# Scan of layer 0: one wide matmul for four rows of decays, denominators kept in PSUM, means on ScalarE and GpSimd, transposes of the unit matrix in waits

## The chip, the cores and the metric

The kernel runs on one core of a Trainium2 chip. The metric is the device time of one execution, in microseconds (us), as a median over executions. The engines are named as the profile names them: PE (TensorE matmuls), PEld (its weight loads), DVE (VectorE), ACT (ScalarE), POOL (GpSimd) and SP (SyncE, which issues the DMAs).

## The reference

Two layers over 1024 tokens of width 1024, and a last RMS norm. Layer 0 projects the normed tokens and then runs two scans over chunks, an SSD (16 heads of 64, state 128, two groups) and an mLSTM (4 heads, keys of 128, values of 256); layer 1 is an attention with differences of two softmaxes. What the change touches is the scan of layer 0:

```python
# SSD, per chunk
decay = where(causal, exp(a_cs[l] - a_cs[s]), 0)
y_diag = einsum('bclsg,bclsgr,bcsgrp->bclgrp', cb, decay, xdt)
y = y_diag + y_off + xs * d_skip ; y = y * silu(z)
yg = y * rsqrt(mean(y * y, per group of 512) + EPS)
# mLSTM, per chunk
m_t = maximum(inter_log, max(d_log))
w_intra = exp(d_log - m_t) ; w_inter = exp(inter_log - m_t)
den = sum(s) + w_inter * (q . n_mem)
h = num / maximum(abs(den), exp(-m_t))
h = h * sigmoid(o_raw) ; h = h * rsqrt(mean(h * h, per head of 256) + EPS)
...
```

## The kernel before

The program has three parts, one behind the other on every engine. `projection_ab` (to 554 us) forms the features, the gates and their tables. `scan_chunks` works through 8 tiles of 128 tokens (two chunks of 64 each) and then forms the first products with the output weights, the "mid products" (units of 24 matmuls, L1370 to L1372). `layer2` does the remaining mid products, the second layer's projection, the attention and the output product. fp32 products are formed as two or three products of fp32r parts, a high part and a low part.

Each engine has its own instruction order, written out by hand, and waits on semaphores. `S["d_h"]`, say, is counted up by DVE (d) for each finished h. A steady tile n of the scan goes like this:

- PE: the rows of decays of the next tile, four groups of four heads (`decay_rows`, L1074). For each head one matmul with a column of `head_sel` broadcast, 128x128 (L1078), puts that head's row of summed decays on all partitions; a matmul in bf16 of 128x512 (L1080) adds the causal mask to the four of them. The columns come from `chunk_tables` (L1084), which DVE runs once a tile: L1085 copies the tile's scalars into `k_g`, L1087 and L1089 the selecting columns. In the same way the rows of the mLSTM's four heads are put on all partitions: the inter-chunk weights (L1263) and the negative maxima (L1266, mask L1268). In between stand transposes of the features (L1055, L1062, L1064, L1070) and the products of keys and queries (L1280).
- DVE `weights`: copies x and b (L1570, L1573), the first half of the decay weights times the products (L1578), the scaled queries (L1586), st (L1593, PE's next step L1311 needs it), gk, the mean of the SSD's squares of the tile before (L1694), half of the turned outputs (L1619), the other half of the weights (L1578), kg (L1607).
- PE `outputs`: the mLSTM's numerators with the denominators as a 257th column (L1311, L1313), transposes of the tile before (L1292), the state's part (L1325), the diagonal part (L1333), then the memory's and the state's new products (L1342, L1349).
- DVE `outputs`: the denominators (L1637 copies them out of PSUM, L1639 forms the absolute value, L1642 the maximum with exp(-m), L1644 the reciprocal), h (L1650, four), the SSD's y (L1657, L1664), the mean of the squares of h (L1669, behind ScalarE's squares L1426), the next tile's tables (L1085 to L1089), the new memory (L1676) and state (L1687).
- ACT: the exponentials of decays (L1405) and of the mLSTM's weights (L1415), squares of h (L1426) and y (L1443), and the norms' scaling (L1433, L1449).
- POOL: x times dt (L1507), x times the skip (L1511), x at the chunk's end (L1515), the decay of the state (L1522, L1527), the power -1/2 of the means of h (L1531), y plus skip (L1534), y times gate (L1540), the power of the means of y (L1542).

In the last tile DVE forms in addition the low parts of the first output units (`low_y`, L1623) and POOL low parts of weights (L1500). In the rows `k_` marks tensors kept over the parts, `s_` those of the scan, `a_` those of layer 2, `c_` those of a tile's input, `b_w`, `b_y_T`, `b_yy` and the like are shared buffers, and `b_ps` is PSUM.

In `layer2`, `step` (L2465) runs the projection's products; before group 0 PE waits for the normed tokens (`h_ok`). The attention's loop ends with two calls of `turn` and the products L2497 and L2510.

## Time and profile before

| | |
|---|---|
| median of three runs | 1554.47 us (1551.89 to 1555.26) |
| profiled execution | 1556.27 us, its span 1554.6 us |
| mean granted clock of TensorE | 0.991 |
| PE, share of the span busy | 97% |
| DVE | 56% |
| ACT | 43% |
| POOL | 36% |
| chain that ended last, PE's share | 47% |
| projection / scan with its mid products / layer 2 | to 553.8 / to 743.5 / to 1554 us |

The shares are means over three very different parts, so the scan is read from its own stretch: the table by stretches gives the granted clock (1.00 is full speed, 2.4 GHz; 0.50 is 1.2 GHz), and the timeline gives who waits for whom. A row of the timeline merges like instructions that follow each other; a matmul's own time is longer than the distance at which the next one starts, so matmuls are priced by distances of starts.

### The profile page before, as it was taken

How to read it: one execution, taken by the hardware profiler on the slowest of the kernel's cores; microseconds unless marked ns; L12 is line 12 of the kernel's file. 1: busy time of each engine (PE TensorE's matmuls, PEld its weight loads, DVE VectorE, ACT ScalarE, POOL GpSimd, SP SyncE). 2: the span in 40 equal slices, each digit the busy share in tenths (PEclk: the TensorE clock that was granted, in tenths of full speed). 3: DMA queues.
4: the chain of work that ended last, by engine and by line, in shares of the span. 5: the costliest groups of instructions: out<-in, count | busy, mean ns of one | idle time of the engine just before them, and what ended most of it. 6: DMA issues, size and time to landing. Idle time of an engine off the chain costs nothing.

```text
span 1554.6 us, 22919 instructions
## 1 busy us (share of the span) xinstructions
PE 1513.2 (97%) x8742; PEld 1290.6 (83%) x8742; DVE 874.0 (56%) x1430; ACT 672.4 (43%) x1320; POOL 558.6 (36%) x324
## 2 busy tenths in 40 slices
PE   9999999999999999999999999999999999998797
PEld 8798988888999988887788877888888888886686
DVE  7674979595944458886353262445544335553633
ACT  6542534454532245555335343345455333656321
POOL 3245444545444336765555321132121014121110
PEclk9999999999999999999999999999999999999999
DMA  5142333232334365684766320031111012113612
GB/s 181 41 125 93 123 95 122 96 122 95 123 109 136 100 197 173 212 267 156 260 208 217 96 84 28 14 95 48 55 51 57 9 35 75 55 35 115 258 68 109
DMA packets 157296, 176.39 MB, mean 113 GB/s; under 512 B 9736, under 2 KB 130824, under 8 KB 156296
## 3 DMA queue, kind: packets, MB, share of 16 engines
q1 hardware_dynamic: 157048, 174.91, 34.7%
q8 instruction: 68, 1.11, 0.3%
q14 instruction: 36, 0.29, 0.1%
q10 hardware_dynamic: 144, 0.07, 0.0%
HBM read 122.46 MB, written 52.43 MB: 113 GB/s over the span
## 4 chain that ended last, share of the span: by engine, by line
PE 47%; DVE 2%; DMA 1%; issue 1%; ACT 0%; POOL 0%; SPq 0%; POOLq 0%; DVEq 0%; ACTq 0%
PE b_ps L2465 22%; PE b_ps L2510 4%; PE b_ps L2485 4%; PE b_ps L2415 3%; PE b_ps L2417 3%; PE b_ps L2416 3%; PE b_ps L2497 2%; PE b_ps L2567 2%; PE b_ps L2569 2%; PE b_ps L2568 2%; DMA b_yy<-z 1%; PE b_ps L2518 1%; PE b_ps L2433 0%; DMA z<-b_y_T 0%; DVE b_y_T L2256 0%
## 5 line engine op out<-in xcount | busy, mean ns | idle before, releaser
L1986 POOL TENSOR_TENSOR b_w<-b_w_raw,b_w 128x1024 fp32r<-128x1024 f32 x66 | 158.0, 2395 | 359.1 <-DVE b_w L2245 253.7
L2465 PE MATMUL b_ps<-a_h_hi,b_w 128*128 128x512 f32 x768 | 265.8, 406 | 2.8 <-DVE a_h_lo L2223 2.8
L402 POOL TENSOR_TENSOR b_w<-b_y_T,b_w 128x1024 fp32r<-128x1024 f32 x54 | 141.3, 2619 | 172.6 <-ACT b_w L460 172.5
L2465 PEld LDWEIGHTS b_ps<-a_h_hi,b_w 128*128 128x128 f32 x768 | 145.3, 189 | 37.0 <-issue 3.9
L2465 PE MATMUL b_ps<-a_h_lo,b_w 128*128 128x512 f32 x384 | 150.8, 393 | 0.0
L956 PE MATMUL b_ps<-p_hi,b_w 128*128 128x512 f32 x384 | 124.1, 396 | 1.8 <-DVE p_lo L628 1.8
L726 DVE SCALAR_TENSOR_TENSOR b_w_raw<-p_out_raw,k_cols,b_w_raw 128x1024 f32<-128x1024 f32 x60 | 119.7, 2002 | 7.8 <-ACT b_w_raw L492 6.4
L2256 DVE CUSTOM_DVE_ANT_0 b_y_T<-b_ps,a_neg_dist 128x128 f32<-128x128 f32 (+5 forms) x96 | 72.2, 777 | 62.8 <-PE b_ps L2485 52.3
L460 ACT CAST b_w<-b_y_T 128x1024 fp32r<-128x1024 f32 x60 | 62.6, 1044 | 90.6 <-PE b_ps L956 51.2
L963 PE MATMUL b_ps<-b_w,p_hi 128*128 128x256 f32 x576 | 101.8, 281 | 0.0
L2107 ACT ACTIVATE b_y_T<-b_y_T,a_nm 128x128 f32<-128x128 f32 (+5 forms) x96 | 75.3, 785 | 52.9 <-DVE a_nm L2256 52.9
L963 PEld LDWEIGHTS b_ps<-b_w,p_hi 128*128 128x128 f32 x576 | 88.4, 190 | 0.4
L402 POOL TENSOR_TENSOR b_w<-b_y_raw,b_w 128x1024 fp32r<-128x1024 f32 x24 | 61.3, 2554 | 76.2 <-ACT b_w L460 76.2
L956 PEld LDWEIGHTS b_ps<-p_hi,b_w 128*128 128x128 f32 x384 | 72.3, 188 | 17.5 <-issue 1.9
L2510 PEld LDWEIGHTS b_ps<-a_v,a_aT 128*128 128x128 f32 x576 | 75.1, 195 | 11.6 <-ACT a_aT L2117 7.0
L2465 PEld LDWEIGHTS b_ps<-a_h_lo,b_w 128*128 128x128 f32 x384 | 73.0, 190 | 11.8
L2465 PE MATMUL b_ps<-b_w,a_h_hi 128*128 128x512 f32 x256 | 80.9, 397 | 1.2 <-ACT a_v L2095 1.2
L2510 PE MATMUL b_ps<-a_v,a_aT 128*128 128x128 f32 x576 | 76.4, 279 | 5.5 <-ACT a_aT L2117 5.5
L2415 PE MATMUL b_ps<-b_w,a_h_hi 128*128 128x512 f32 x208 | 81.4, 391 | 0.0
L2025 POOL TENSOR_TENSOR a_rs<-a_rs,a_half 128x4 f32<-128x4 f32 x16 | 17.3, 1083 | 177.8 <-DVE a_rs L2282 177.8
L2417 PE MATMUL b_ps<-b_w,a_h_lo 128*128 128x512 f32 x208 | 81.1, 390 | 0.0
L2416 PE MATMUL b_ps<-b_w,a_h_hi 128*128 128x512 f32 x208 | 81.0, 389 | 0.0
(410 smaller groups left out, 3611.6 us busy)
## 6 DMA issues: line engine op xcount, KB each, us to landing
b_y_T<-in_ab_w_in SPq DMA_DIRECT2D x33, 512.0 KB, 4.4
b_w_raw<-in_ab_w_out SPq DMA_DIRECT2D x32, 512.0 KB, 4.2
b_w_raw<-in_c_w_in SPq DMA_DIRECT2D x32, 512.0 KB, 4.1
tok<-p_out_raw SPq DMA_DIRECT2D x48, 256.0 KB, 2.3
feat<-b_w_raw SPq DMA_DIRECT2D x20, 512.0 KB, 2.9
c_fe<-feat SPq DMA_DIRECT2D x7, 1280.0 KB, 6.8
yt<-b_y_T SPq DMA_DIRECT2D x8, 1024.0 KB, 9.7
b_y_raw<-yt SPq DMA_DIRECT2D x32, 256.0 KB, 4.2
```

Source lines behind the costliest of these rows:

```text
L402: gp.tensor_tensor(w_lo[s % SLOTS][:, :, :], operand(n, split_of(n, p))[:, :, :], w_hi[s % SLOTS][:, :, :].bitcast(F32), ALU.subtract).the ...
L726: dve.scalar_tensor_tensor(out=acc, in0=raw(j), scalar=cols[:, c:c + 1], in1=acc, op0=ALU.mult, op1=ALU.add).then_inc(S["tapped" if j < CO ...
L956: mm = pe.matmul(out[:, :], x0[:, k, fs], x1[:, k, :], start=opens and k == 0 and i == 0, stop=closes and k == HK - 1 and i == 2)
L963: mm = pe.matmul(out[:, h * HB:(h + 1) * HB], x0[:, k, ts], x1[:, k, :], start=k == 0 and i == 0, stop=k == HK - 1 and i == 2)
L1986: gp.tensor_tensor(w_lo[:, w, :], w_raw[u % W_RAW][:, :], w_hi[:, w, :].bitcast(F32), ALU.subtract).then_inc(S["l_wlo"], 1)
L2107: nc.scalar.activation(s[:, 0:W], s[:, 0:W], ACT.Exp, bias=nm[n % 2][:, j:j + 1], scale=-1.0, accum_out=sm[n % 2][:, j:j + 1]).then_inc(S[ ...
L2256: dve.tensor_tensor_reduce(s[:, 0:W], score[j][:, at:at + W], neg_dist[:, SEQ - W:SEQ], -SLOPES[h], 3e38, ALU.add, ALU.min, nm[n % 2][:, j ...
L2415: pe.matmul(ps[:, bank, :], y_hi(u)[:, ts], w_hi[:, w, c], start=(k == 0), stop=False)
L2416: pe.matmul(ps[:, bank, :], y_hi(u)[:, ts], w_lo[:, w, c], start=False, stop=False)
L2417: mm = pe.matmul(ps[:, bank, :], y_lo(u)[:, ts], w_hi[:, w, c], start=False, stop=(k == AB_OUT_T - 1))
L2465: mm = pe.matmul(o, x, y, start=(k == 0 and q == 0), stop=(k == KT - 1 and q == 2))
L2510: mm = pe.matmul(ps[:, 5, 0:DA_V], aT[:, k, :], v[:, k, (h % 4) * DA_V:(h % 4 + 1) * DA_V], start=(k == 0), stop=(k == t))
```

## The change

1. One matmul of 128x512 takes the place of four of 128x128 wherever rows of four heads are put on all partitions (L1078, L1263, L1266). The right-hand side becomes block-diagonal: four copies of the rows next to each other, of which copy i keeps only the rows of heads 4q + i (`dec_bd`, `ml_bd`; the mask is `of_four`), so that one column that selects a whole group of four heads gives four rows at once. The selecting columns shrink from 16 and 8 to 4 and 2. `dec_bd` is formed by two DVE operations in the projection (one copy before), `ml_bd` by one at the scan's start, for which PE waits then.
2. The denominators are worked out in PSUM: max(-den, exp(-m)), then max with den in place, then the reciprocal from PSUM; three DVE operations for four.
3. DVE's order: the first L1578 goes behind st and gk. In the last tile the low part of unit 1 goes from the weights to behind y.
4. The means: ScalarE scales inside its squares, GpSimd adds EPS before its powers, and DVE's two operations (L1669, L1694) go. Each square of h waits for its own h and no more for all four.
5. PE gets 62 transposes of the unit matrix into a PSUM bank that nobody reads then (`idle_turns`): 14 and 10 in tile 0 of the scan, 14 before layer 2's group 0, and 12 before each of the attention's last two turns.
6. Buffers: the mLSTM's gate cells get their own, and some scratch of the gates moves; these move no instruction.

```diff
+                dve.tensor_reduce(quads, ident[:, :].rearrange("p (a h) -> p a h", h=ML_HEADS), AX.X, ALU.add).then_inc(S["heads_ok"], 1)
+                dve.tensor_reduce(keep["of_four"][:, :], ident[:, :].rearrange("p (a h) -> p h a", h=ML_HEADS), AX.X, ALU.add
+                                  ).then_inc(S["heads_ok"], 1)
+                dve.wait_ge(S["heads_ok"], 1)
+                of_rows = quads.rearrange("p (r s q) -> p s r q", s=2, q=4)
+                dve.tensor_tensor(keep["heads_of"][:, :, :], of_rows[:, 0, :, :], of_rows[:, 1, :, :], ALU.add).then_inc(S["heads_ok"], 1)
+                of_rows = quads.rearrange("p (b s c) -> p s c b", b=2, s=2)
+                dve.tensor_tensor(keep["cells_of"][:, :, :], of_rows[:, 0, :, :], of_rows[:, 1, :, :], ALU.add).then_inc(S["heads_ok"], 1)
...
-                chain(dve.tensor_copy(dec_rows, g_ps["rows"][:, 2 * P:4 * P].rearrange("p (j t) -> p j t", j=2)))
+                dve.wait_ge(S["heads_ok"], 4)
+                for j in (0, 1):
+                    chain(dve.tensor_tensor(dec_bd[:, j, :, :], mid(g_ps["rows"][:, (2 + j) * P:(3 + j) * P], 4),
+                                            last(keep["of_four"][:, :], P), ALU.mult))
...
 def decay_rows(pe, ps, keep, par, q, S):
     bank = 4 + q % 2
-    for k in range(4):
-        h = 4 * q + k
-        pe.matmul(ps[:, bank, k * P:(k + 1) * P], keep["head_sel"][:, h:h + 1].broadcast_to([P, P]),
-                  keep["dec_rows"][:, par * P:(par + 1) * P], start=(k == 0), stop=False, skip_group_check=True)
+    pe.matmul(ps[:, bank, :], keep["head_sel"][:, q:q + 1].broadcast_to([P, P]), keep["dec_bd"][:, par, :],
+              start=True, stop=False, skip_group_check=True)
     pe.matmul(ps[:, bank, :], keep["ident_bf"][:, :], mid(keep["later"][:, :], 4), start=False, stop=True,
               skip_group_check=True).then_inc(S["p_acs"], 1)
...
-        gates = lambda n, par, i: gz[par][:, i, :] if behind_first(n) else chunk["first_gz"][i]
+        gates = lambda n, par, i: (gz[par][:, i, :] if i < 2 else cell_gate[par]) if behind_first(n) else chunk["first_gz"][i]
...
+        ml_bd = ahead["w"][:, 1, 2, 0:BLK]
...
-                    pe.wait_ge(S["ml_rows"], 4 * 16)
+                    pe.wait_ge(S["d_mlbd"], 1)
                 pe.wait_ge(S["cell_ok"], n + 1)
-                row_of = lambda b, h: keep["cell_sel"][:, ML_HEADS * b + h:ML_HEADS * b + h + 1].broadcast_to([P, P])
+                rows_of = lambda b: keep["cell_sel"][:, b:b + 1].broadcast_to([P, P])
                 if behind_first(n):
                     pe.wait_ge(S["d_cmem"], n * 4)
-                    for k in range(4):
-                        mm = pe.matmul(ps[:, 7, k * P:(k + 1) * P], row_of(1, k), keep["ml_rows"][:, :], start=True, stop=True)
-                    mm.then_inc(S["p_wint"], 1)
-                for k in range(4):
-                    pe.matmul(ps[:, 6, k * P:(k + 1) * P], row_of(0, k), keep["ml_rows"][:, :], start=(k == 0), stop=False,
-                              skip_group_check=True)
+                    pe.matmul(ps[:, 7, :], rows_of(1), ml_bd, start=True, stop=True).then_inc(S["p_wint"], 1)
+                pe.matmul(ps[:, 6, :], rows_of(0), ml_bd, start=True, stop=False, skip_group_check=True)
                 pe.matmul(ps[:, 6, :], ident_bf[:, :], mid(later[:, :], 4), start=False, stop=True,
                           skip_group_check=True).then_inc(S["p_negm"], 1)
                 if not behind_first(n):
                     decays(n, par, 2)
+                    pe.wait_ge(S["d_xtok"], 2)
+                    idle_turns(0, 14)
                     decays(n, par, 3)
+                    idle_turns(0, 10)
                     return
...
+            def idle_turns(bank, count):
+                for _ in range(count):
+                    pe.transpose(ps[:, bank, 0:P], ident[:, :], ident[:, :])
...
-                act.wait_ge(S["d_h"], n * 4 + 4)
-                act.wait_ge(S["d_meanm"], n + 0)
+                act.wait_ge(S["l_meanm"], n + 0)
                 act.wait_ge(S["a_sqy"], n * 2)
                 for h in range(ML_HEADS):
+                    act.wait_ge(S["d_h"], n * 4 + (h + 1))
                     act.wait_ge(S["a_sqm"], n * 4 + h)
-                    nc.scalar.activation(x_sq[:, 0:ML_V], y[:, D + h * ML_V:D + (h + 1) * ML_V], ACT.Square,
+                    nc.scalar.activation(x_sq[:, 0:ML_V], y[:, D + h * ML_V:D + (h + 1) * ML_V], ACT.Square, scale=ML_V ** -0.5,
                                          accum_out=ssq[:, 2 + h:3 + h]).then_inc(S["a_sqm"], 1)
...
-                act.wait_ge(S["d_meany"], n + 0)
+                act.wait_ge(S["l_meany"], n + 0)
                 for k in (0, 1):
                     act.wait_ge(S["a_sqy"], n * 2 + k)
-                    nc.scalar.activation(x_sq[:, :], y[:, k * 512:(k + 1) * 512], ACT.Square,
+                    nc.scalar.activation(x_sq[:, :], y[:, k * 512:(k + 1) * 512], ACT.Square, scale=512 ** -0.5,
                                          accum_out=ssq[:, k:k + 1]).then_inc(S["a_sqy"], 1)
...
-                gp.wait_ge(S["d_meanm"], n + 1)
+                gp.wait_ge(S["a_sqm"], n * 4 + 4)
+                gp.tensor_tensor(rms[:, 2:6], ssq[:, 2:6], eps[:, :], ALU.add).then_inc(S["l_meanm"], 1)
+                gp.wait_ge(S["l_meanm"], n + 1)
                 gp.tensor_tensor(rms[:, 2:6], rms[:, 2:6], half[:, 0:4], ALU.pow).then_inc(S["l_rstdm"], 1)
...
-                gp.wait_ge(S["d_meany"], n + 1)
+                gp.wait_ge(S["a_sqy"], n * 2 + 2)
+                gp.tensor_tensor(rms[:, 0:2], ssq[:, 0:2], eps[:, 0:2], ALU.add).then_inc(S["l_meany"], 1)
+                gp.wait_ge(S["l_meany"], n + 1)
                 gp.tensor_tensor(rms[:, 0:2], rms[:, 0:2], half[:, 0:2], ALU.pow).then_inc(S["l_rstdy"], 1)
...
-                ssd_weights(0)
...
-                means()
+                ssd_weights(0)
...
                     low_y(0)
-                    low_y(1)
...
-                dve.tensor_copy(den[:, :], ps[:, 4:8, ML_V:VW].rearrange("p h a -> p (h a)")).then_inc(S["d_den"], 1)
-                dve.wait_ge(S["d_den"], n * 4 + 1)
-                dve.scalar_tensor_tensor(out=den2[:, :], in0=den[:, :], scalar=-1.0, in1=den[:, :],
+                den_ps = ps[:, 4:8, ML_V:VW].rearrange("p h a -> p (h a)")
+                dve.scalar_tensor_tensor(out=den[:, :], in0=den_ps, scalar=-1.0, in1=g[:, T_EMT:T_EMT + ML_HEADS],
                                          op0=ALU.mult, op1=ALU.max).then_inc(S["d_den"], 1)
-                dve.wait_ge(S["d_den"], n * 4 + 2)
-                dve.tensor_tensor(den2[:, :], den2[:, :], g[:, T_EMT:T_EMT + ML_HEADS], ALU.max).then_inc(S["d_den"], 1)
-                dve.wait_ge(S["d_den"], n * 4 + 3)
-                dve.reciprocal(den[:, :], den2[:, :]).then_inc(S["d_den"], 1)
-                dve.wait_ge(S["d_den"], n * 4 + 4)
+                dve.wait_ge(S["d_den"], n * 3 + 1)
+                dve.tensor_tensor(den_ps, den_ps, den[:, :], ALU.max).then_inc(S["d_den"], 1)
+                dve.wait_ge(S["d_den"], n * 3 + 2)
+                dve.reciprocal(den[:, :], den_ps).then_inc(S["d_den"], 1)
+                dve.wait_ge(S["d_den"], n * 3 + 3)
...
-                dve.wait_ge(S["a_sqm"], n * 4 + 4)
-                dve.tensor_scalar(rms[:, 2:6], ssq[:, 2:6], 1.0 / ML_V, EPS, ALU.mult, ALU.add).then_inc(S["d_meanm"], 1)
-                if not is_last(n):
+                if is_last(n):
+                    low_y(1)
+                else:
                     next_tables()
...
-            def ssd_means(n):
-                dve.wait_ge(S["a_sqy"], n * 2 + 2)
-                dve.tensor_scalar(rms[:, 0:2], ssq[:, 0:2], 1.0 / 512, EPS, ALU.mult, ALU.add).then_inc(S["d_meany"], 1)
+            dve.wait_ge(S["ml_rows"], 4 * 16)
+            dve.tensor_tensor(ml_bd.rearrange("p (h t) -> p h t", t=P), mid(keep["ml_rows"][:, :], 4), last(keep["of_four"][:, :], P),
+                              ALU.mult).then_inc(S["d_mlbd"], 1)
             weights(0, 0, 0)
             def body(n, par, prior):
                 outputs(n, par, prior, lambda: tables(n + 1, prior + par))
-                weights(n + 1, 1 - par, prior + par, lambda: ssd_means(n), lambda: turn(n, 0, par, prior))
+                weights(n + 1, 1 - par, prior + par, lambda: turn(n, 0, par, prior))
...
-            ssd_means(TILES - 1)
...
                     if g == 0:
+                        idle_turns(bank, 14)
                         pe.wait_ge(S["h_ok"], TILES)
...
             for n in range(-1, N + 1):
+                if n >= N - 1:
+                    pe.wait_ge(S["a_fe"], G)
+                    idle_turns(7, 12)
...
-            keep |= dict(heads_of=sel[:, 0:64].rearrange("p (r h) -> p r h", h=SSD_HEADS),
-                         cells_of=sel[:, 64:128].rearrange("p (c h) -> p c h", c=TILES), head_sel=sel[:, 128:128 + SSD_HEADS],
-                         cell_sel=sel[:, 144:144 + 2 * ML_HEADS], ml_rows=sel[:, 152:152 + P])
+            keep |= dict(heads_of=sel[:, 0:16].rearrange("p (r q) -> p r q", q=4),
+                         cells_of=sel[:, 16:32].rearrange("p (c b) -> p c b", c=TILES), head_sel=sel[:, 32:36],
+                         cell_sel=sel[:, 36:38], ml_rows=sel[:, 40:40 + P])
```

PE, tile 0 of the scan, from its first products of keys and queries (L1254) to the diagonal products; `k_sel` are the selecting columns, before:

```order
L1254 MATMUL b_ps<-b_w_raw,b_y_raw 128x128 x4
L1266 MATMUL b_ps<-k_sel 128x128 x4
L1268 MATMUL b_ps<-k_later,k_ident_bf 128x512
L1078 MATMUL b_ps<-k_dec_rows,k_sel 128x128 x4
L1080 MATMUL b_ps<-k_later,k_ident_bf 128x512
L1078 MATMUL b_ps<-k_dec_rows,k_sel 128x128 x4
L1080 MATMUL b_ps<-k_later,k_ident_bf 128x512
L1311 MATMUL b_ps<-c_va,s_st 128x257 x4
```

and now:

```order
L1262 MATMUL b_ps<-b_w_raw,b_y_raw 128x128 x4
L1271 MATMUL b_ps<-b_w,k_sel 128x512
L1272 MATMUL b_ps<-k_later,k_ident_bf 128x512
L1084 MATMUL b_ps<-k_dec_bd,k_sel 128x512
L1086 MATMUL b_ps<-k_later,k_ident_bf 128x512
L1293 MATMUL b_ps<-k_ident 128x128 x14
L1084 MATMUL b_ps<-k_dec_bd,k_sel 128x512
L1086 MATMUL b_ps<-k_later,k_ident_bf 128x512
L1293 MATMUL b_ps<-k_ident 128x128 x10
L1323 MATMUL b_ps<-c_va,s_st 128x257 x4
```

Each four became one of four times the width, and two runs of turns (L1293) stand before and behind the last group. In the later tiles the groups change in the same way and no turns come in.

DVE, a steady tile, from the copies of x to kg, before:

```order
L1570 COPY s_x_tok<-b_ps 128x512 x2
L1573 COPY s_b_tok<-b_ps 128x256
L1578 TENSOR_TENSOR s_wt<-s_dec,b_ps 128x1024
L1586 TENSOR_TENSOR s_qs<-c_fe,b_ps 128x512
L1589 COPY s_c_dec<-b_ps 128x4
L1593 SCALAR_TENSOR_TENSOR s_st<-b_ps,s_wm 128x512
L1596 TENSOR_SCALAR s_gk<-s_wm 128x4
L1694 TENSOR_SCALAR s_rms<-s_ssq 128x2
L1619 TENSOR_TENSOR b_y_T<-b_ps,b_y_T 128x512 x2
L1578 TENSOR_TENSOR s_wt<-s_dec,b_ps 128x1024
L1607 TENSOR_TENSOR s_kg<-b_ps,s_gk 128x512
```

and now:

```order
L1588 COPY s_x_tok<-b_ps 128x512 x2
L1591 COPY s_b_tok<-b_ps 128x256
L1602 TENSOR_TENSOR s_qs<-c_fe,b_ps 128x512
L1605 COPY s_c_dec<-b_ps 128x4
L1609 SCALAR_TENSOR_TENSOR s_st<-b_ps,s_wm 128x512
L1612 TENSOR_SCALAR s_gk<-s_wm 128x4
L1596 TENSOR_TENSOR s_wt<-s_dec,b_ps 128x1024
L1634 TENSOR_TENSOR b_y_T<-b_ps,b_y_T 128x512 x2
L1596 TENSOR_TENSOR s_wt<-s_dec,b_ps 128x1024
L1622 TENSOR_TENSOR s_kg<-b_ps,s_gk 128x512
```

The first half of the weights moved from before the queries to behind gk, and the mean is gone. DVE, the same tile, from the denominators to the memory, before:

```order
L1637 COPY s_den<-b_ps 128x4
L1639 SCALAR_TENSOR_TENSOR s_den<-s_den 128x4
L1642 TENSOR_TENSOR s_den<-s_den,k_g 128x4
L1644 RECIPROCAL s_den<-s_den 128x4
L1650 SCALAR_TENSOR_TENSOR s_y<-b_ps,s_den,c_gz 128x256 x4
L1657 TENSOR_TENSOR s_t<-b_ps,k_g 128x512 x2
L1664 TENSOR_TENSOR s_y<-b_ps,s_t 128x512 x2
L1669 TENSOR_SCALAR s_rms<-s_ssq 128x4
L1085 TENSOR_SCALAR k_g<-k_table 128x56
L1087 TENSOR_SCALAR k_sel<-k_sel 128x16
L1089 TENSOR_SCALAR k_sel<-k_sel 128x8
L1676 SCALAR_TENSOR_TENSOR s_cmem<-s_cmem,s_c_dec,b_ps 128x257 x4
```

and now:

```order
L1654 SCALAR_TENSOR_TENSOR s_den<-b_ps,k_g 128x4
L1657 TENSOR_TENSOR b_ps<-b_ps,s_den 128x4
L1659 RECIPROCAL s_den<-b_ps 128x4
L1665 SCALAR_TENSOR_TENSOR s_y<-b_ps,s_den,c_gz 128x256 x4
L1672 TENSOR_TENSOR s_t<-b_ps,k_g 128x512 x2
L1679 TENSOR_TENSOR s_y<-b_ps,s_t 128x512 x2
L1091 TENSOR_SCALAR k_g<-k_table 128x56
L1093 TENSOR_SCALAR k_sel<-k_sel 128x4
L1095 TENSOR_SCALAR k_sel<-k_sel 128x2
L1690 SCALAR_TENSOR_TENSOR s_cmem<-s_cmem,s_c_dec,b_ps 128x257 x4
```

The denominators read and write PSUM, and the three table operations (L1091 to L1095 now) follow y with nothing between.

## Rows read from the trace of the kernel before

**Rows 1.** The page, busy time of each engine (share of the span) and instructions.

```profile
PE 1513.2 (97%) x8742; PEld 1290.6 (83%) x8742; DVE 874.0 (56%) x1430; ACT 672.4 (43%) x1320; POOL 558.6 (36%) x324
```

**Rows 2.** Table by stretches: stretch, length, busy PE, PEld, DVE, ACT, POOL, clock, DMA.

```profile
559.20:566.00 6.80, 6.14 (x21) 4.93 (x20) 4.61 (x11) 1.78 (x7) 3.10 (x2) 0.50 1.14 344
...
716.30:723.00 6.70, 6.17 (x15) 4.89 (x16) 3.33 (x8) 4.68 (x14) 3.60 (x3) 0.50 0.69 249
...
904.00:907.30 3.30, 3.30 (x8) 2.57 (x9) 2.11 (x4) 2.35 (x4) 1.13 (x3) 0.50 0.47 191
...
1443.30:1450.00 6.70, 5.95 (x28) 5.45 (x26) 3.94 (x6) 2.13 (x7) 0.00 (x0) 0.50 0.56 222
```

**Rows 3.** Timeline, PE's mask matmuls of a tile: start, length, then [idle before <-releaser].

```profile
656.06 0.39 PE L1080 MATMUL b_ps<-k_later,k_ident_bf 128*128 128x512 bf16 x1
...
656.69 0.39 PE L1080 MATMUL b_ps<-k_later,k_ident_bf 128*128 128x512 bf16 x1
...
658.86 0.39 PE L1080 MATMUL b_ps<-k_later,k_ident_bf 128*128 128x512 bf16 x1
...
660.56 0.39 PE L1080 MATMUL b_ps<-k_later,k_ident_bf 128*128 128x512 bf16 x1
```

**Rows 4.** Timeline, PE at the last tile and in the mid products.

```profile
711.69 3.75 PE L1333 MATMUL b_ps<-s_xdt,s_wt 128*128 128x64 f32 x32 [0.93 <-DVE b_y_T L1619]
...
716.83 0.80 PE L1370 MATMUL b_ps<-b_w,b_yy 128*128 128x512 f32 x1 [1.39 <-DVE s_y L1650]
...
723.24 0.40 PE L1370 MATMUL b_ps<-b_w,b_yy 128*128 128x512 f32 x1
...
723.47 0.40 PE L1371 MATMUL b_ps<-b_w,b_yy 128*128 128x512 f32 x1
```

**Rows 5.** Timeline, DVE's denominators and POOL, a steady tile and the last one.

```profile
646.88 1.93 POOL L1515 TENSOR_TENSOR s_xe<-s_xdt,s_dec 128x1024 f32<-128x1024 f32 x1
...
648.07 0.77 DVE L1639 SCALAR_TENSOR_TENSOR s_den<-s_den 128x4 f32<-128x4 f32 x1
...
712.60 2.27 DVE L1642 TENSOR_TENSOR s_den<-s_den,k_g 128x4 f32<-128x4 f32 x1
```

**Rows 6.** Timeline, DVE's tables, memory and state, POOL beside them, and PE behind.

```profile
534.23 2.64 POOL L402 TENSOR_TENSOR b_w<-b_y_T,b_w 128x1024 fp32r<-128x1024 f32 x1 [3.34 <-ACT b_w L460]
534.53 2.38 DVE L1085 TENSOR_SCALAR k_g<-k_table 128x56 f32<-128x56 f32 x1
...
653.83 0.19 DVE L1085 TENSOR_SCALAR k_g<-k_table 128x56 f32 x1 [0.25 <-issue]
...
654.29 1.66 DVE L1676 SCALAR_TENSOR_TENSOR s_cmem<-s_cmem,s_c_dec,b_ps 128x257 f32<-128x257 f32 x4
...
654.63 2.37 POOL L1534 TENSOR_TENSOR s_y<-s_y,s_x_tok 128x1024 f32<-128x1024 f32 x1
...
655.87 1.28 DVE L1687 TENSOR_TENSOR s_state<-s_state,b_ps 128x512 f32<-128x512 f32 x2
...
657.79 0.38 PE L1062 MATMUL b_ps<-k_ident,c_fe 128*128 128x128 f32 x2
```

**Rows 7.** Timeline, DVE's kg and PE's state part that follows in its bank.

```profile
644.52 0.69 DVE L1607 TENSOR_TENSOR s_kg<-b_ps,s_gk 128x512 f32<-128x512 f32 x1
...
646.92 1.88 PE L1325 MATMUL b_ps<-s_state,c_fe 128*128 128x512 f32 x4
```

**Rows 8.** Timeline, PE in tile 0.

```profile
558.86 0.84 PE L1078 MATMUL b_ps<-k_dec_rows,k_sel 128*128 128x128 f32 x4 [1.64 <-ACT s_dec L1405]
...
560.81 3.77 PE L1311 MATMUL b_ps<-c_va,s_st 128*128 128x257 f32 x8 [0.66 <-DVE s_st L1593]
```

**Rows 9.** L1028 alone by stretches (PE, PEld, clock, DMA); timeline, PE at layer 2's group 0.

```profile
2.00:4.80 2.80, 2.80 (x15) 2.80 (x14) 1.00 0.99 333
...
6.10:6.90 0.80, 0.80 (x7) 0.55 (x5) 1.00 1.02 399
...
903.86 0.69 PE L2465 MATMUL b_ps<-a_h_hi,b_w 128*128 128x512 f32 x1 [2.85 <-DVE a_h_lo L2223]
```

56 lines of the change are left out of this document (31 added, 25 removed).

## The prediction

> **What bounds the kernel now.** I read the page first: PE is busy 97% of the span, DVE 56% and POOL 36% [rows 1], so time is gained by taking work from PE, by ending its waits, or by raising its clock. Then the table by stretches, for the clock: four stretches run at a granted clock of 0.50, the 1.2 GHz level: in tile 0 of the scan, after its last tile, at layer 2's first product group, and near the end [rows 2]. Each comes behind a pause of PE, such as the 1.64 us at 558.86 [rows 8] or the 2.85 us at 903.86 [rows 9]. Last the timeline of a steady tile, for who waits for whom: PE follows itself there almost without a pause, so that each matmul removed is time.
>
> **Rows of decays, rows of cells (part 1).** A group of four 128x128 matmuls L1078 and the 128x512 of L1080 takes 0.63 us, from the start of one L1080 to the next, 656.06 to 656.69 [rows 3]. The fp32r matmuls of 128x512 at full clock start 0.23 us apart (723.24, 723.47) [rows 4]; L1080 with its 512 columns gets the same price, so a new group is 0.46 us and gives back 0.17. Between L1080 at 658.86 and L1080 at 660.56 lie 1.70 us [rows 3]: four L1263, four L1266, L1268 and one group. Less the group of 0.63 that is 1.07, and new three matmuls at 0.23, 0.69: 0.38 us. A tile has four groups: 4 x 0.17 + 0.38 = 1.06 us, all on PE, and seven tiles have both kinds (tile 0 has no L1263): **7.4 us**. The price rests on a dense PE, so it can shrink to what DVE or ACT let through, below. The masked copies are built by DVE during the projection, where DVE is not the bound [rows 1], and one more at the start of the scan, in which PE waits for ACT anyway: 0, at most 0.7 us for one 128x512 operation (L1607, 0.69) [rows 7].
>
> **Denominators (part 2).** L1639 and L1642 have all their inputs in SBUF. L1639 took 0.77 us at 648.07 and ended at 648.84, where POOL's L1515 (646.88, 1.93) ended, 648.81; L1642 at 712.60 took 2.27 [rows 5]. With the inputs in PSUM I price the three that stay at 0.2 us each, so the four outputs h come some 0.7 us sooner in a steady tile. No PE wait names them there, so this is 0 in seven tiles, covered by PE's own matmuls; if that cover were gone it could give 0.7 us a tile. In the last tile PE does wait, below.
>
> **Order on DVE and the last tile (part 3).** In the last tile PE waits 0.93 us at 711.69 for DVE's L1619, which stood behind the two low parts, and 1.39 us at 716.83 for h [rows 4], which stood behind L1642's 2.27 us. The change puts the second low part behind y and takes the stalls from the denominators, so h is done before PE comes there: 2.3 us. Then PE has no pause in front of the mid products, and the 15 matmuls that filled 6.17 us at a clock of 0.50 [rows 2] would take 15 x 0.23 = 3.45: 2.7 us. Together **5.0 us**, between 2.3 (clock falls anyway) and 5.0. Next late is the low part of unit 1, but unit 0 has 24 matmuls, 24 x 0.23 = 5.5 us, ahead of it, which cover it. In the steady tile the first L1578 goes behind st and so delays kg (L1607) by about 1.1 us. Before, kg ends at 645.21, and PE's L1325, which follows in the same bank, starts at 646.92 [rows 7]: 1.7 us, less 1.1 leaves 0.6. So 0, with little to spare.
>
> **Means (part 4).** The scale inside ScalarE's squares costs nothing I can see, and squares that wait for each h alone start earlier. GpSimd gets two additions of 128x4 and 128x2 a tile; the trace has none such. Their bounds are 0 and the 1.93 us of a 128x1024 operation with two SBUF inputs [rows 5]; 0.2 is the value I take, since there are 256 times fewer columns. POOL is idle 64% [rows 1] and waits for these squares: 0 on the path. What DVE loses by it matters more: L1669, in which it waited for the squares, is gone, and the tables (L1085 to L1089) come right behind y.
>
> **What that brings with it.** POOL's L1534 (128x1024, 2.37 us) needs y and the powers. Before, the powers came late, and L1534 started at 654.63, behind the tables, which began at 653.83 and cost 0.19 for L1085 [rows 6]. Now the powers are done before y, and L1534 can start about 0.1 us behind y, while the three tables run. They read SBUF alone, and L1085 once took 2.38 us, at 534.53, where POOL's L402 (534.23, 2.64) ran until 536.87 [rows 6]. y would end at about 653.1 on the old time axis (0.7 sooner); L1534 would run from 653.2 to 655.5 and hold the tables so long. L1676 (1.66) and L1687 (1.28) follow [rows 6], to 658.5. PE's L1062 waits for that state; without the stall it would start at 657.79 [rows 6] less two groups' 0.34, 657.45. So PE loses 1.1 us in each of six tiles, and I take 0.8 in tile 0: **7.4 us**. The other bound is 0, if the tables get ahead of L1534. I take the stall, since L1085's 2.38 us is the nearest row there is.
>
> The Trainium skill, page "SBUF — State Buffer", section "SBUF: two separate sides", says of the ports that VectorE and GpSimd share that whichever operation starts first holds them for the whole instruction. By that rule, the trace agrees in L1085's 2.38 us, and L1085 itself would slip through while L1087 and L1089 are open.
>
> **Turns of the unit matrix (part 5).** 62 transposes of 128x128 are added. At the program's start PE did nothing but L1028's transposes: 15 in 2.80 us first, 0.19 each, later 7 in 0.80, 0.11 each [rows 9]. I read that as the clock's rise under transposes alone. If they keep it up: in tile 0 the eight L1311, 3.77 us at 0.50 [rows 2, 8], halve, 1.9 us, and some of the other 2.4 us of that stretch: **2.3 us**, between 0 and 3.0 (half of its 6.14). In layer 2 the eight matmuls of 3.30 us halve [rows 2]: **1.6 us**; the 14 turns lie in PE's wait of 2.85 us [rows 9] and take 14 x 0.11 = 1.5, so they cost nothing, but 1.3 us of pause stay behind them, so 0 is the other bound. At the end the 28 matmuls of 5.95 us [rows 2] give at most 3.0; the second twelve turns lie in no wait and cost 12 x 0.11 = 1.3, up to 2.3 at 0.19. **1.6 us**, between -2.3 and 1.7.
>
> **The sum.** Without the stall 7.4 + 5.0 + 2.3 + 1.6 + 1.6 = 17.9 us. With it, 17.9 - 7.4 = 10.5 us. The profiled execution took 1556.27 us, 1554.6 of them its span and 1.67 around it, which nothing here touches; with the stall it would be 1545.8. It stands 1.8 us above the median of 1554.47, so on the median the forecast is **1544.0 us**.
>
> **Rivals.** (a) No stall: the tables are through before L1534. For it: L1085 can start in y's tail, before the semaphore reaches POOL. Against it: three operations, of which the last starts some 0.3 us behind y. 1554.47 - 17.9 = **1536.6 us**.
> (b) The turns don't keep the clock. Of the sum 2.3 + 1.6 + 1.6 go, and 1.3 us of turns at the end are paid: 6.8 us less. With the stall 1550.8, without it 1543.4. For it: 0.50 was reached with pauses of 1.6 us, and pauses of 1.3 are left. Against it: L1028's spacing.
> The Trainium skill, page "TensorE: Matmul & The Clock Gate", section "Part 4: PE-mode transpose", speaks against the change: it says that transposes do not count as PE busy for the clock's gate. By that rule rival (b) would hold; L1028's rows speak against the rule.
> (c) Slower: kg. If DVE reaches kg later than I think, by a stall of st, gk or the first L1578 beyond the 0.6 us of slack, PE's L1325 waits in seven tiles. It must lose all of 10.5 us: 0.6 + 10.5/7 = 2.1 us a tile is the point from which it decides; a whole L1534 of 2.37 us in front of it would make 7 x (2.37 - 0.6) = 12.4, so **1556.4 us** and, from 3 us on, 1560.8. Against it: L1578 and L1607 read one input from PSUM, as L1650 does, and I saw no stall of such operations.
> (d) The change does what it says, but DVE or ACT follow PE so closely that the 1.06 us of a tile come back as waits for st: 10.5 - 7.4 = 3.1, **1551.4 us**. Against it: DVE's 56% [rows 1].
>
> **How the numbers follow.** Stall and clock held 0.43; (a) 0.32; (b) 0.15, two thirds of it with the stall; (c) 0.03; (d) 0.07. The range should leave out 2 in 10 at most: from (a) with some microseconds of the remaining pauses falling better, 1533, to (b) with the stall, 1551. A measurement of this kernel can't tell under about 0.2% (3.1 us) from no change. Faster by more than that means below 1551.4: 0.43 + 0.32 + 0.14 and half of (d), 0.92. Within it 0.05, slower 0.03.
>
> **What would show it.** Right: groups of L1084 and L1086 0.46 us apart; L1093 or L1095 of about 2.3 us that ends with POOL's L1550; PE waiting about 1 us for the state at its group transposes; no wait in front of the mid products, at a clock of 1.00. Wrong: table operations of 0.2 us (then 1536.6 holds); clocks of 0.50 behind the turns (rival b); PE waiting for kg at its state matmuls (rival c); PE waiting for st by over 1 us a tile (rival d). The forecast as a whole is wrong if PE's clock falls in places where it did not before, since one such stretch costs 1.6 to 3 us here.

## The result

| | before | changed |
|---|---|---|
| median of four runs | 1553.32 us | 1540.42 us (1539.99 to 1542.90) |
| ratio of the runs, 95% interval | | 0.9919 (0.9902 to 0.9935) |
| profiled execution, its span | 1556.27, 1554.6 us | 1542.90, 1541.1 us |
| PE, busy time | 1513.2 us | 1506.8 us |

The kernel became 0.8% faster, 12.9 us by the medians and 13.4 by the two profiled executions. That lies inside the predicted range; the point, 1544.0, was 3.6 us too slow. Where the gain came from is another matter: one term did not happen, one came out with the wrong sign in this execution, and one was not in the sum. Of all executions behind this document one is left out, of the kernel with the low part early (1681.21 us at a granted clock of 0.847), and that kernel's median is of its other five.

The same matmul can be found in both traces, and the difference of its two starts tells how far the changed kernel is ahead there. Read at eight places:

| place | before | changed | ahead by | since the last place |
|---|---|---|---|---|
| first product of the scan (L1254, now L1262) | 554.84 | 556.25 | -1.41 | -1.41 |
| first rows of tile 1 (L1078, L1084) | 571.79 | 570.76 | 1.03 | 2.44 |
| diagonal products of the last tile (L1333, L1345) | 711.69 | 702.70 | 8.99 | 7.96 |
| first mid product (L1370, L1382) | 716.83 | 706.19 | 10.64 | 1.65 |
| fifteenth mid product (L1372, L1384) | 722.97 | 709.50 | 13.47 | 2.83 |
| layer 2's first transposes behind group 0 (L2433, L2446) | 911.00 | 895.82 | 15.18 | 1.71 |
| layer 2's product behind the next transposes (L2465, L2484) | 919.87 | 905.71 | 14.16 | -1.02 |
| first output product (L2567, L2589) | 1454.76 | 1442.19 | 12.57 | -1.59 |

The page of the changed kernel, busy time of each engine as in [rows 1]:

```profile
PE 1506.8 (98%) x8663; PEld 1273.0 (83%) x8663; DVE 865.0 (56%) x1409; ACT 673.4 (44%) x1320; POOL 564.8 (37%) x341
```

PE lost 79 instructions net (the 62 turns are among those that are left) and 6.4 us of busy time, in which a lower clock counts too. The other 7.1 us of the span's 13.5 are time in which PE waited before. The table by stretches of the changed kernel (the columns of [rows 2]), in tile 0, behind the last tile, at group 0 and near the end:

```profile
559.20:566.00 6.80, 6.27 (x45) 5.24 (x43) 5.99 (x12) 3.67 (x15) 4.90 (x3) 1.00 1.12 332
...
706.00:723.00 17.00, 17.00 (x86) 14.27 (x86) 10.31 (x12) 9.12 (x16) 9.84 (x8) 1.00 0.57 189
...
890.00:895.00 5.00, 4.76 (x21) 3.96 (x22) 2.58 (x5) 3.51 (x6) 1.72 (x5) 1.00 0.57 199
...
1414.00:1417.40 3.40, 3.40 (x12) 2.82 (x11) 0.35 (x1) 3.37 (x6) 0.00 (x0) 0.50 0.66 265
...
1424.20:1427.60 3.40, 3.40 (x15) 2.38 (x16) 0.41 (x1) 0.90 (x4) 3.32 (x3) 0.50 0.00 0
```

The first three stretches, which stood at 0.50 before [rows 2], now run at full clock. Near the end the long one is gone, and two of 3.4 us stand 29 and 19 us earlier in the trace, which is 15 and 5 us earlier in the work, since the kernel is 14 us ahead there. They follow pauses of 2.48 and 2.35 us. The first pause was there before, 2.49 us long, and had not brought the clock down; in place of the second the kernel before had waits of 1.55 and 0.80 us. The timeline of a steady tile on PE, the mask matmuls that answer to [rows 3]:

```profile
650.75 0.39 PE L1086 MATMUL b_ps<-k_later,k_ident_bf 128*128 128x512 bf16 x1
...
651.21 0.39 PE L1086 MATMUL b_ps<-k_later,k_ident_bf 128*128 128x512 bf16 x1
...
653.22 0.39 PE L1086 MATMUL b_ps<-k_later,k_ident_bf 128*128 128x512 bf16 x1
...
654.38 0.39 PE L1086 MATMUL b_ps<-k_later,k_ident_bf 128*128 128x512 bf16 x1
```

A group takes 0.46 us (0.63 before), and from the third group's mask to the fourth's it is 1.16 us (1.70 before). The same tile on DVE and POOL, which answers to [rows 6] and [rows 7]:

```profile
640.43 0.69 DVE L1622 TENSOR_TENSOR s_kg<-b_ps,s_gk 128x512 f32<-128x512 f32 x1
...
641.76 1.88 PE L1337 MATMUL b_ps<-s_state,c_fe 128*128 128x512 f32 x4
...
647.20 0.69 DVE L1679 TENSOR_TENSOR s_y<-b_ps,s_t 128x512 f32<-128x512 f32 x1 [0.28 <-PE b_ps L1345]
...
647.81 0.18 DVE L1091 TENSOR_SCALAR k_g<-k_table 128x56 f32 x1
647.90 0.16 DVE L1093 TENSOR_SCALAR k_sel<-k_sel 128x4 fp32r x1
647.97 2.38 POOL L1550 TENSOR_TENSOR s_y<-s_y,s_x_tok 128x1024 f32<-128x1024 f32 x1 [0.29 <-DVE s_y L1679]
647.98 0.16 DVE L1095 TENSOR_SCALAR k_sel<-k_sel 128x2 fp32r x1
...
649.07 1.66 DVE L1690 SCALAR_TENSOR_TENSOR s_cmem<-s_cmem,s_c_dec,b_ps 128x257 f32<-128x257 f32 x4 [0.93 <-PE b_ps L1354]
```

Here the stall of the forecast is looked for in vain: POOL's L1550 starts 0.08 us behind y, as reckoned, but the three tables have started at 647.81, 647.90 and 647.98, and none takes more than 0.18 us. DVE then waits 0.93 us for PE, and PE waits for nothing in this tile. kg ends at 641.12, 0.64 us before L1337, the slack that the prediction left it.

The -1.02 of the table is a wait of PE behind group 0:

```profile
905.71 0.70 PE L2484 MATMUL b_ps<-b_w,a_h_hi 128*128 128x512 f32 x2 [0.77 <-DVE b_yy L2246]
```

In the kernels with turns in group 0 PE loses 0.2 to 0.3 us at this place in nine traces and 1.0 us in two, this one among them. ScalarE has waited 0.77 us for a DMA in front of the operations that lead to b_yy (at 896.65), and 0.21 us in the kernel below that leaves out the end's turns, where PE loses 0.26. So part of what is gained at group 0 is taken back; why that DMA comes later is open.

### The profile page after: what moved, and what is told of

Read it like the earlier page. It is cut to its first block, busy times and chain, and to the rows that moved or that the text cites. A ratio compares the mean times of both kernels' runs of the same rounds, so it can differ in the third digit from the quotient of the medians.

```text
span 1541.1 us, 22792 instructions
## 1 busy us (share of the span) xinstructions
PE 1506.8 (98%) x8663; PEld 1273.0 (83%) x8663; DVE 865.0 (56%) x1409; ACT 673.4 (44%) x1320; POOL 564.8 (37%) x341
## 4 chain that ended last, share of the span: by engine, by line
PE 47%; DVE 2%; DMA 1%; issue 1%; ACT 1%; POOL 0%; SPq 0%; POOLq 0%; DVEq 0%; ACTq 0%
PE b_ps L2484 22%; PE b_ps L2529 4%; PE b_ps L2504 4%; PE b_ps L2428 3%; PE b_ps L2430 3%; PE b_ps L2429 3%; PE b_ps L2516 2%; PE b_ps L2589 2%; PE b_ps L2591 2%; PE b_ps L2590 2%; DMA b_yy<-z 1%; PE b_ps L2537 1%; DVE a_h_lo L2236 0%; DMA z<-b_y_T 0%; DVE b_y_T L2269 0%
## 5 line engine op out<-in xcount | busy, mean ns | idle before, releaser
L2484 PE MATMUL b_ps<-a_h_hi,b_w 128*128 128x512 f32 x768 | 265.3, 406 | 1.2 <-DVE a_h_lo L2236 1.2
L2484 PEld LDWEIGHTS b_ps<-a_h_hi,b_w 128*128 128x128 f32 x768 | 144.9, 189 | 35.2 <-issue 3.9
L2484 PE MATMUL b_ps<-a_h_lo,b_w 128*128 128x512 f32 x384 | 150.5, 392 | 0.0
L2484 PE MATMUL b_ps<-b_w,a_h_hi 128*128 128x512 f32 x256 | 80.8, 397 | 2.0 <-ACT a_v L2108 1.2
L2484 PEld LDWEIGHTS b_ps<-a_h_lo,b_w 128*128 128x128 f32 x384 | 72.8, 189 | 11.8
L971 PE MATMUL b_ps<-b_w,p_lo 128*128 128x256 f32 x288 | 80.0, 278 | 0.0
```

The costliest lines, as they stand in the source:

```text
L971: mm = pe.matmul(out[:, h * HB:(h + 1) * HB], x0[:, k, ts], x1[:, k, :], start=k == 0 and i == 0, stop=k == HK - 1 and i == 2)
L2484: mm = pe.matmul(o, x, y, start=(k == 0 and q == 0), stop=(k == KT - 1 and q == 2))
```

## The experiments

Each is the changed kernel, or the kernel before where its name says so, with one edit. Ratios are to the kernel before, with their 95% intervals; the changed kernel has 0.9919, and 0.001 is 1.55 us. The intervals are some 3 to 6 us wide, so where a difference is smaller, its place in the two traces decides, not the ratio.

### The tables a little later

```diff
                 else:
+                    for i in range(4):
+                        dve.reciprocal(late[:, 48 * i:48 * i + 48], half[:, 0:1].broadcast_to([P, 48]))
                     next_tables()
```

> The changed kernel with four short reciprocals (128x48, of a constant, into a buffer that nobody reads) between y and the tables, so that the tables start some 0.3 us later, behind the start of POOL's L1550 instead of just ahead of it. Theory 1 (the stall of the prediction is real and only missed by 0.1 us: the first of the two that starts goes through, the other is held): a table operation takes about 2.2 us, PE loses 1.0 us in each of seven tiles, 6 to 8 us slower than the changed kernel. Rival (L1550 does not hold such small operations; the 2.38 us of the projection's table operation has another reason): table operations of 0.2 us, no more than 1 us slower.

Measured: 1548.43 us, ratio 0.9970 (0.9956 to 0.9983), 7.9 us slower than the changed kernel. Its timeline in the tile that stands above:

```profile
652.07 1.38 DVE L1688 RECIPROCAL s_late<-k_half 128x48 f32<-128x48 f32 x4
652.23 2.35 POOL L1551 TENSOR_TENSOR s_y<-s_y,s_x_tok 128x1024 f32<-128x1024 f32 x1 [0.30 <-DVE s_y L1680]
...
653.36 1.26 DVE L1091 TENSOR_SCALAR k_g<-k_table 128x56 f32 x1
654.55 0.15 DVE L1093 TENSOR_SCALAR k_sel<-k_sel 128x4 fp32r x1
...
654.69 1.65 DVE L1693 SCALAR_TENSOR_TENSOR s_cmem<-s_cmem,s_c_dec,b_ps 128x257 f32<-128x257 f32 x4
```

L1091 took 1.26 us and ended at 654.62, where POOL's operation ended (652.23 + 2.35 = 654.58); the reciprocals beside the same operation were not held to its end: the first of them started ahead of it, and the other three, which started behind it, took no longer (0.39 us each by their records, against 0.44). Matched to the changed kernel, PE loses 1.0 to 1.2 us in each of seven tiles. The reciprocals took longer than I had reckoned, 1.38 us in all. Without the stall the tables would have been done at 653.7, and DVE could have begun L1693 then, 0.4 us later than in the changed kernel when both are measured from y; with it L1693 is 1.4 us late. So some 1.0 us of each tile's delay is the stall's. The stall is real; what was wrong was on which side of it the kernel falls.

### Part 1 undone: four narrow matmuls

```diff
-    pe.matmul(ps[:, bank, :], keep["head_sel"][:, q:q + 1].broadcast_to([P, P]), keep["dec_bd"][:, par, :],
-              start=True, stop=False, skip_group_check=True)
+    for k in range(4):
+        pe.matmul(ps[:, bank, k * P:(k + 1) * P], keep["head_sel"][:, q:q + 1].broadcast_to([P, P]),
+                  keep["dec_bd"][:, par, k * P:(k + 1) * P], start=(k == 0), stop=False, skip_group_check=True)
...
```

and the same for the two products with `ml_bd`.

> The changed kernel with four matmuls of 128 columns for each one of 512, on the same block-diagonal rows. Theory 1 (PE is dense in the steady tile, so matmul time is span): slower by 7 x 1.05 = 7.4 us, 1547.8, each tile 1.0 to 1.1 us longer. Rival (DVE or ACT follow so closely that part of it is covered): 2 to 5 us slower, with shorter waits of PE for st.

Measured: 1548.85 us, ratio 0.9961 (0.9947 to 0.9974), 6.5 us slower than the changed kernel, against 7.4 expected. From tile 0's diagonal products to the last tile's it gains 1.1 us on the kernel before, where the changed kernel gains 8.6: 7.6 us. PE is dense there, and the price by starts of matmuls holds. The last 0.9 us are inside the interval, and this kernel's profiled execution had no stretch at 0.50 near the end.

### Part 2 undone: the denominators in SBUF

```diff
-                dve.scalar_tensor_tensor(out=den[:, :], in0=den_ps, scalar=-1.0, in1=g[:, T_EMT:T_EMT + ML_HEADS],
+                dve.tensor_copy(den[:, :], den_ps).then_inc(S["d_den"], 1)
+                dve.wait_ge(S["d_den"], n * 4 + 1)
+                dve.scalar_tensor_tensor(out=den2[:, :], in0=den[:, :], scalar=-1.0, in1=den[:, :],
...
```

> The changed kernel with the denominators copied to SBUF first, in four operations as before. Theory 1: steady tiles lose nothing, as PE's diagonal products cover h; in the last tile the maximum is held until POOL's low parts end (706.8 in the changed kernel's profile), h ends about 2.5 us after PE wants the first mid product: 2.5 us slower, up to 4.3 if the pause brings a clock of 0.50. Rival: h is on the path in every tile and the cost is 7 x 0.7 = 5 us and more.

Measured: 1542.94 us, ratio 0.9938 (0.9925 to 0.9950), 2.9 us slower. Up to the last tile its matmuls start within 0.5 us of the changed kernel's. The timeline of the last tile, DVE, POOL and PE:

```profile
701.92 4.64 POOL L1515 TENSOR_TENSOR b_w<-b_w_raw,b_w 128x1024 fp32r<-128x1024 f32 x2
701.93 2.36 DVE L1657 SCALAR_TENSOR_TENSOR s_den<-s_den 128x4 f32<-128x4 f32 x1
...
704.32 2.27 DVE L1660 TENSOR_TENSOR s_den<-s_den,k_g 128x4 f32<-128x4 f32 x1
...
708.55 0.50 PE L1383 MATMUL b_ps<-b_w,b_yy 128*128 128x512 f32 x1 [2.38 <-DVE s_y L1668]
```

Two operations of 128x4 take 4.63 us between them, one for each of POOL's two. PE waits 2.38 us, and the clock falls to 0.50 for the next 3.4 us: the sixteenth mid product starts 4.0 us later than in the changed kernel. As forecast, it is the last tile alone.

### Part 3 undone, in two halves

```diff
                     low_y(0)
+                    low_y(1)
                     return
...
-                if is_last(n):
-                    low_y(1)
-                else:
+                if not is_last(n):
                     next_tables()
```

> The changed kernel with the low part of unit 1 back in the last tile's weights, ahead of the turned outputs. Theory 1: PE waits 0.9 us for the turned outputs at the diagonal products again, nothing else: 0.5 to 1 us slower, h still in time. Rival: the whole wait in front of the mid products comes back: 2.3 us and a stretch at 0.50, up to 5 us slower.

Measured: 1545.55 us, ratio 0.9943 (0.9926 to 0.9959), 3.7 us slower with an interval of about 2.5 us on either side. The timeline of PE in its last tile:

```profile
704.20 3.76 PE L1345 MATMUL b_ps<-s_xdt,s_wt 128*128 128x64 f32 x32 [1.20 <-DVE b_y_T L1635]
```

PE is 1.5 us behind the changed kernel there and stays so; the mid products follow without a wait, at full clock. The trace thus shows 1.5 us for this half, somewhat over the 0.9 expected, and the first theory; another 1.8 us came behind group 0, where its trace has one more stretch at 0.50 than the changed kernel's (1435.3 to 1438.7).

```diff
+                ssd_weights(0)
+
                 if behind_first(n):
                     dve.wait_ge(S["p_wint"], n + 0)
...
-                ssd_weights(0)
                 turned()
```

> The changed kernel with the first half of the decay weights back in front of the queries on DVE. Theory 1 (in a steady tile st waits for PE's key products in either order, 1.4 us in the changed kernel): nothing in steady tiles, at most 1 us in tile 0, where st comes behind the weights. Rival (st comes later by part of 1.2 us in every tile): 2 to 7 us slower, with PE waiting for st at its numerators.

Measured: 1542.81 us, ratio 0.9930 (0.9911 to 0.9949). From the projection to 900 us no matmul starts more than 0.5 us from its start in the changed kernel, tile 0 included. The move of the first half of the weights is worth nothing that the trace shows. The six executions of this kernel also show what the clock does to one and the same kernel: two at a mean granted clock of 0.998 took 1538.8 and 1539.0 us, four at 0.994 to 0.996 took 1542.6 to 1545.4.

### Part 4 undone: the means on DVE

```diff
-                gp.wait_ge(S["a_sqm"], n * 4 + 4)
-                gp.tensor_tensor(rms[:, 2:6], ssq[:, 2:6], eps[:, :], ALU.add).then_inc(S["l_meanm"], 1)
-                gp.wait_ge(S["l_meanm"], n + 1)
+                gp.wait_ge(S["d_meanm"], n + 1)
...
+                dve.wait_ge(S["a_sqm"], n * 4 + 4)
+                dve.tensor_scalar(rms[:, 2:6], ssq[:, 2:6], 1.0 / ML_V, EPS, ALU.mult, ALU.add).then_inc(S["d_meanm"], 1)
```

> The changed kernel with the means formed by DVE as before and ScalarE's squares unscaled, each still waiting for its own h only. Theory 1 (squares end before y, so DVE doesn't wait for them any more, and nothing of part 4 but the early squares is on a path): within 1 us of the changed kernel. Rival 1: the mean in front of the tables pushes these behind L1550's start: stalls of 2 us, 6 to 8 us slower. Rival 2: the powers come later and with them y times gate and the squares of y, PE waits for the norm: 2 to 5 us slower.

Measured: 1539.69 us, ratio 0.9919 (0.9900 to 0.9937), the ratio of the changed kernel. Its timeline behind y:

```profile
647.65 0.16 DVE L1681 TENSOR_SCALAR s_rms<-s_ssq 128x4 f32<-128x4 f32 x1
647.71 0.18 DVE L1091 TENSOR_SCALAR k_g<-k_table 128x56 f32 x1
...
647.88 1.03 POOL L1545 TENSOR_TENSOR s_rms<-s_rms,k_half 128x4 f32<-128x4 f32 x1 [1.08 <-DVE s_rms L1681]
648.88 2.37 POOL L1548 TENSOR_TENSOR s_y<-s_y,s_x_tok 128x1024 f32<-128x1024 f32 x1
```

The mean takes 0.16 us and waits for nothing. Moving the means has no price and no gain. In this order POOL's large operation starts 0.9 us later, so the tables are farther from the stall than in the changed kernel.

### Part 5: the turns, left out in steps and alone

```diff
                 if not behind_first(n):
                     decays(n, par, 2)
-                    pe.wait_ge(S["d_xtok"], 2)
-                    idle_turns(0, 14)
                     decays(n, par, 3)
-                    idle_turns(0, 10)
...
                     if g == 0:
-                        idle_turns(bank, 14)
...
-                if n >= N - 1:
-                    pe.wait_ge(S["a_fe"], G)
-                    idle_turns(7, 12)
```

All of it in one kernel:

> The changed kernel without any of the 62 turns. Theory 1 (turns hold the clock): the stretches at 0.50 in tile 0 and at layer 2's group 0 come back, slower than the kernel without the end's turns alone by 2.3 + 1.5 = 3.8 us. Rival (turns do nothing for the clock; the stretches went because the waits in front changed): the same time as without the end's turns, clocks of 1.00 in both places.

the last three lines alone in the next:

> The changed kernel (1540.4 us) without the 24 turns before the attention's last two turns. Theory 1 (the turns near the end cost what they take and hold no clock: in the changed kernel two stretches of 3.4 us at a clock of 0.50 stood there, of which the later lasted into the first turns): faster by 1 to 3 us, 1537.5 to 1539.5. Theory 2 (they keep the clock up in the last pauses, as predicted): slower by 1 to 2 us, and a stretch of some 7 us at 0.50 comes back behind the pause before the last but one turn, as in the kernel before.

and all the lines of the first cut added to the kernel before, without the rest of the change:

> The kernel before with the 62 turns alone. Theory 1: tile 0 and group 0 run at full clock, 2.3 + 1.5 us gained, the end open by 2 us either way: 1548 to 1551 against 1553.3. Rival (the turns hold no clock): 1553 to 1555, with 0.50 in both places. The stretch of 0.50 behind the scan's last tile stays in both, since no turns are there.

Measured: without any 1541.68 us, ratio 0.9917 (0.9901 to 0.9932); without the end's 1542.66, 0.9917 (0.9903 to 0.9931); alone 1549.56, 0.9969 (0.9956 to 0.9982), 4.8 us faster than the kernel before. The stretches of the kernel without any turn, in tile 0 and at group 0, then those of the kernel without the end's, near the end, in tile 0 and at group 0:

```profile
560.00:567.00 7.00, 6.08 (x31) 5.04 (x31) 4.88 (x10) 2.47 (x10) 3.79 (x2) 0.76 1.12 344
887.00:900.00 13.00, 10.15 (x46) 8.17 (x45) 7.45 (x9) 8.70 (x12) 6.19 (x8) 0.87 0.48 163
```

```profile
1431.00:1438.00 7.00, 6.16 (x28) 5.35 (x26) 4.06 (x6) 2.60 (x8) 0.00 (x0) 0.51 0.42 169
560.00:567.00 7.00, 6.62 (x46) 5.46 (x45) 6.19 (x13) 3.78 (x15) 4.48 (x3) 1.00 1.12 342
887.00:900.00 13.00, 11.76 (x68) 9.97 (x66) 8.32 (x10) 9.02 (x13) 6.46 (x8) 1.00 0.48 163
```

Without turns 3.4 us of each stretch are at 0.50 again; with them it is at 1.00. One trace could be chance here, but all eleven kernels with these turns show 1.00 in both places, and all three without (the kernel before, the padded one below, and this one) show 0.50 in both. In the traces the turns are worth 0.9 us in tile 0, where the stretch came back at half its old length, and 1.6 us up to the transposes behind group 0, where it came back at its full 3.4 us: this kernel gains nothing there on the kernel before, the one with the turns 1.63. Near the end both theories have a part: without its turns a stretch of some 7 us at 0.51 is back behind a pause of 2.0 us, and what it costs is what the turns cost. A stretch at 0.50 behind this third pause stands in all four traces without the end's turns, and in two of the nine that have them where the changed kernel does. The ratios can't tell these kernels from the changed one. In the kernel before, where all pauses were as long as they had been, the turns alone gave 4.8 us, of the 5.5 that the prediction gave to its three terms; its trace has 2.2 us in tile 0, 1.6 at group 0 and 1.3 at the end. The stretch behind the last tile, where no turns are, stayed in part (0.50 from 715.0 to 718.4 in its trace).

### Where the projection's parts lie

In the kernel before, with 128 unused bytes ahead of the selecting columns:

```diff
+                        space=o.sb("space", [P, 32]),
                         sel=o.sb("sel", [P, (KT + KT // 2) * GATES], F32R), g=o.sb("g", [P, T_USED]), cols=o.sb("cols", [P, COLUMNS]),
```

> The kernel before with an unused buffer of 128 bytes a partition ahead of the selecting columns, so that the projection's parts lie 128 bytes further on, as they do in the changed kernel modulo 4096. In every kernel with the change so far the projection's 128x512 products with these parts as weights start 3 to 5 ns further apart, 2.4 us up to 383 us of the span, and a part of it is won back later; in the two kernels without it they don't. Theory 1 (the place in SBUF sets this): the same drift of 1 to 2.4 us in this kernel, 1 to 1.5 us slower than the kernel before. Rival (it comes with the change's own work, as the masked rows on DVE): no drift, the time of the kernel before.

and in the changed kernel the other way round, with the mask in another buffer's padding:

```diff
-                        tri=o.sb("tri", [P, P]), half=o.sb("half", [P, ML_HEADS]),
+                        tri=o.sb("tri", [P, P]), half=o.sb("half", [P, 2 * ML_HEADS]),
...
-                        of_four=o.sb("of_four", [P, 4]), space=o.sb("space", [P, 24]),
...
+            keep |= dict(half=keep["half"][:, 0:4], of_four=keep["half"][:, 4:8])
```

> The changed kernel with the mask of_four in the padding of another small buffer and without the unused 96 bytes, so that the projection's parts lie exactly 4096 bytes from their place in the kernel before, and no longer 4224. Theory 1 (their place modulo 4096 sets the rate of the projection's products): no drift of 1 to 2.4 us against the kernel before in the projection, 1 to 1.5 us faster than the changed kernel, about 1539. Rival (any move of these buffers costs the same): the drift stays, no difference.

Measured: the padded kernel before 1554.95 us, ratio 1.0006 (0.9995 to 1.0016); the moved changed kernel 1540.97 us, 0.9919 (0.9901 to 0.9936). In times neither differs from its original. In the traces both do. The scan's first product, in the kernel before, padded, in the changed kernel, and moved:

```profile
554.84 1.13 PE L1254 MATMUL b_ps<-b_w_raw,b_y_raw 128*128 128x128 f32 x8 [1.07 <-PEq L170]
```

```profile
556.07 1.13 PE L1254 MATMUL b_ps<-b_w_raw,b_y_raw 128*128 128x128 f32 x8 [1.07 <-PEq L170]
```

```profile
556.25 1.13 PE L1262 MATMUL b_ps<-b_w_raw,b_y_raw 128*128 128x128 f32 x8 [1.39 <-PEq L170]
```

```profile
555.02 1.13 PE L1262 MATMUL b_ps<-b_w_raw,b_y_raw 128*128 128x128 f32 x8 [1.39 <-PEq L170]
```

The padded kernel drifts behind its original along the same course as the changed kernel does: 1.0 us at 94, 2.0 at 356, and 1.2 at the end of the projection. The moved one does not drift. So about 1.2 of the 1.4 us that the changed kernel loses up to the scan are the place of its buffers, and no work of the change; 0.18 us are left in the moved kernel. Why a place costs that much is open.

The padded kernel shows something else. Its program is that of the kernel before, and its waits in the last tile are the same 0.93 and 1.39 us, but behind them its clock stays up:

```profile
717.20 0.50 PE L1370 MATMUL b_ps<-b_w,b_yy 128*128 128x512 f32 x1 [1.39 <-DVE s_y L1650]
...
716.30:723.00 6.70, 5.80 (x25) 4.80 (x26) 3.33 (x9) 4.31 (x14) 3.31 (x2) 1.00 0.74 258
```

So the 6.7 us at 0.50 in [rows 2] belong to one execution of the kernel before, and not to each of them. Near the end it is the other way round: the padded kernel has stretches at 0.50 behind all three pauses (from 1425.7, 1435.9 and 1446.2, each 3.4 us long), where the trace of the kernel before has one.

### The turns near the end in other waits

```diff
-                if n >= N - 1:
+                if n in (N - 2, N - 1):
                     pe.wait_ge(S["a_fe"], G)
                     idle_turns(7, 12)
...
+                if n == N - 4:
+                    pe.wait_ge(S["a_fe"], G - 1)
+                    idle_turns(bank_of(G - 2), 12)
                 if 0 <= n - 1 < N:
                     values(n - 1)
```

on top of the moved buffers.

> As the last, with the turns near the end put elsewhere: twelve in each of three waits (before the value products of the last but four, before the last but two and before the last but one turn), and none before the last turn, where they stand in no wait. Theory 1 (turns in a wait hold the clock and cost nothing): no stretch at 0.50 between 1405 and 1450, and 1.3 us of turns less on the path: 2 to 4 us faster than the kernel with the buffers moved alone. Rival (the pauses near 1411 and 1421 don't always drop the clock, and the turns make the pauses' ends later): within 1 us of it.

Measured: 1539.04 us (1537.21 to 1540.64), ratio 0.9907 (0.9889 to 0.9926). The stretch that held two at 0.50 in the changed kernel:

```profile
1405.00:1450.00 45.00, 37.03 (x234) 30.46 (x231) 23.71 (x41) 21.37 (x42) 6.55 (x5) 1.00 0.65 238
```

The clock stays at 1.00, and its span is 1537.1 us, 4.0 less than the changed kernel's. That alone shows little, since four kernels with the end's turns in their old place have no 0.50 there either (narrow matmuls, denominators in SBUF, weights first, means on DVE), two of them with a span of 1537.0. The mean granted clocks say more: 0.997 or 0.998 in all five executions, against 0.995 or 0.996 in five of the moved kernel's six. By the times it is 1.9 us faster than the moved kernel, which the intervals don't separate. It is the fastest version measured here, and not shown to be faster than the changed one.

## Why the prediction was right, and where it was not

**Rows of decays and cells: right.** 1.06 us a tile was forecast. From tile 1 to the last tile the lead grows by 1.03 us a tile over six tiles, and the kernel with narrow matmuls gives 7.6 us back in the trace and 6.5 in the times, against 7.4.

**Denominators, and the last tile: right for the waits, by luck for the clock.** No steady tile needed them, and the last tile's wait in front of the mid products is gone; undone, the wait is 2.38 us. The terms of 5.0 us measured 1.65 up to the first mid product and 2.83 by its clock, and about 1 us more, for the wait of 0.93, lies ahead of the diagonal products. But the 2.83 are a gain on the one execution that was profiled: the padded kernel, with the same two waits, has no stretch at 0.50 there, and the kernel before with the turns alone half of it. Against those two executions the term is nothing, or about half; the prediction's lower bound, 2.3, has the waits alone. Of the two causes of the wait, the low part took 1.5 us and the denominators 2.4 when each was undone alone.

**Order on DVE, means: right, at nothing.** kg kept 0.64 us of slack in a steady tile, so rival (c) had no footing; only in tile 0 does PE wait for kg, 0.36 us at 564.03. The two kernels with these edits undone run as the changed one does up to 900 us.

**The stall: wrong.** This is the step that took the forecast from 17.9 to 10.5 us: "L1534 can start about 0.1 us behind y, while the three tables run ... and hold the tables". The start was right to some hundredths. But the tables follow y on the same engine without any semaphore, 0.09 us apart, and had started, the last of them within 0.01 us of POOL's operation. L1085's 2.38 us in the projection came from an operation that started 0.30 us behind POOL's, so it was no measure for one that starts with it. I took a price from a row without asking whether its order of starts was the one I reckoned with; rival (a) had the right reason. The term of 7.4 us is nothing. With the tables behind POOL's start by 1.1 us the price is what was forecast, 1.0 to 1.2 us a tile.

The Trainium skill, page "SBUF — State Buffer", section "SBUF: two separate sides", names the operation that starts first as the one that keeps the ports. The two traces agree with it, 0.18 us on the one side and 1.26 us up to POOL's end on the other.

**Turns: right twice; at the end the opposite of the forecast, by stretches that the turns don't touch.** Tile 0 gained 2.44 us (2.3 forecast), some 0.2 of it by the wide matmuls (2.2 with narrow ones), and group 0 1.71 (1.6), of which the wait for b_yy takes 1.02 back. The prediction read the turns' hold on the clock from L1028's spacing alone; the clock column of [rows 9] says 1.00 in both of its stretches, so those rows didn't show it, and the experiments do. At the end 1.6 us of gain were forecast, and from 919 us to the first output product 1.59 us were lost. The timeline of PE there, in the changed kernel:

```profile
1413.48 1.67 PE L2529 MATMUL b_ps<-a_v,a_aT 128*128 128x128 f32 x8 [2.48 <-ACT a_aT L2130]
...
1423.32 0.88 PE L2516 MATMUL b_ps<-a_ident,b_y_T 128*128 128x128 f32 x6 [2.35 <-DVE b_y_T L2283]
...
1435.23 1.47 PE L2453 MATMUL b_ps<-a_ident 128*128 128x128 f32 x12
```

The two stretches at 0.50 follow the first two pauses; the turns come only behind them, at 1429.08 and 1435.23. The kernel before had the first of these pauses too, 2.49 us at 1427.42, and went through at full clock; the padded one had it at 2.35 us and fell to 0.50. So whether a pause brings the clock down is not a property of the pause alone. In the five kernels with these turns whose traces have no 0.50 between 1405 and 1450, PE gains 1.1 to 1.5 us on the kernel before from 919 us to the first output product, close to the 1.6; in those that have such stretches it loses 1.6 to 4.1. The loss is that of the execution, and no run shows that the change makes such stretches likelier. The prediction named this, "PE's clock falls in places where it did not before", and gave it no term. The turns before the last turn stand in no wait and take 1.3 us by distances of starts (1435.23 to the next product's 1436.54), as reckoned.

The Trainium skill, page "TensorE: Matmul & The Clock Gate", section "Part 4: PE-mode transpose", holds that transposes don't count as PE busy in the same way for the clock. The traces differ from it: tile 0 and group 0 run at 1.00 with the turns and fall to 0.50 without.

**What the sum left out.** The projection's 1.4 us. The new buffers `of_four`, with its padding, and `dec_bd` moved those behind them by 4224 bytes, and the prediction has no term for the place of a buffer.

Put together: 17.9 us without the stall, less the 1.4 of the projection and 3.2 at the end (1.59 lost where 1.6 were to be gained) makes 13.3; the profiled executions differ by 13.4. Two more differences of the traces are not in this sum, the 1.02 us lost behind group 0 and 0.9 gained behind the first output product, and they cancel. The forecast of 10.5 was near because two errors of 4.6 us together stood against one of 7.4. That is luck: the prediction's sign for rival (a), table operations of 0.2 us, came true, and the 1536.6 us that went with it did not.

## What to carry to other kernels

A row that shows a stall is a price for the order of starts it was taken in. Before it goes into a sum, ask for both operations what releases them: work that follows on its own engine is ahead of work that a semaphore lets go, by about 0.1 us here, and that was enough. A change that removes a wait from in front of a chain of small operations, which another engine's operation can hold up, can be safe by such a margin alone, so keep the chain directly behind its predecessor. And where new buffers are put ahead of others, look at the places of those behind them, since a dense stage can lose over half a per cent without an instruction of it being touched (2.4 us of 383 here). And before a stretch at a lower clock is priced from one trace, look whether a second execution has it.

## What was not expected of the hardware

The place of the projection's parts in SBUF: moved by 4224 bytes (or by 128) instead of 4096 (or 0), its products of 128x512 with these parts as weights start 3 to 5 ns further apart, 2.4 us up to 383 us of the span, of which half is won back later. The kernels with the changed kernel's places drift so, and so does the padded kernel before; the kernel before, the same with turns alone, and the two moved ones don't: their scan begins between 554.84 and 555.05 us, that of the others between 555.93 and 556.62.

The reciprocals that delayed the tables were not held by POOL's operation, though they read and write SBUF alone, while L1091 behind them was; both are short DVE operations on SBUF. L1095 in the changed kernel started 0.01 us behind POOL's operation by the records and wasn't held; whether by the order of starts or because it is never held, no run tells. And pauses of the same length on PE brought the clock to 0.50 in some executions and not in others with the same code there (1.39 us in front of the mid products, 2.35 to 2.49 near the end), so a single trace is one draw of it.
